# Delta-rule core: the next round's setup inside this round's tail, and other homes in PSUM

## What is computed

```
G = cumsum(g);  decay = where(incl, exp(G_i - G_j), 0)
kb = k * beta
a = where(strict, (kb @ k^T) * decay, 0)
rhs = concat[v * beta, kb * exp(G)]
u, w = solve((I + a), rhs)            # unit lower triangular
intra = (q @ k^T) * decay
step:  v_new = u - w @ state
       o = (q * exp(G)) @ state + intra @ v_new
       state = state * exp(g_last) + k_dec^T @ v_new
```

## Time and profile before

| | |
|---|---|
| median of 3 runs | 2420.59 us (2418.37 to 2424.03) |
| the profiled execution, its own time | 2420.17 us |
| its span | 2418.2 us |
| busy: PE, DVE, ACT, POOL | 1996.5, 928.4, 632.6, 32.5 us |
| the core's four rounds in the span | from 123.5 to about 333 us |
| HBM read | 639.21 MB, 265 GB/s over the span |

### The profile page before, as it was taken

How to read it: one execution, slowest core, us unless ns; L and a number is a source line. 1 busy time by engine, 2 the same in 40 slices (tenths; PEclk the granted TensorE clock), 3 DMA queues, 4 the chain that set the end, 5 groups by cost and what they waited for, 6 DMA issues and landing times.

```text
span 2418.2 us, 34547 instructions
## 1 busy us (share of the span) xinstructions
PE 1996.5 (83%) x14552; PEld 1375.0 (57%) x14552; DVE 928.4 (38%) x1676; ACT 632.6 (26%) x1065; POOL 32.5 (1%) x51
## 2 busy tenths in 40 slices
PE   8887888999988998999987666666999987666665
PEld 7765656887755886988853222222978843222222
DVE  4655563767555566544521000002544521000001
ACT  3321234441124443464420000001364420000000
POOL 0100000000000000000000000000000000000000
PEclk9998899999998999999989888888999978888888
DMA  9301024776954576442559999999542569999997
GB/s 326 118 25 36 2 71 140 253 282 235 362 209 174 199 288 220 167 148 106 229 242 425 427 426 426 427 425 410 215 148 116 218 251 426 426 427 426 426 427 312
DMA packets 150882, 641.86 MB, mean 265 GB/s; under 512 B 9374, under 2 KB 30904, under 8 KB 117622
## 3 DMA queue, kind: packets, MB, share of 16 engines
q1 hardware_dynamic: 144474, 637.13, 66.7%
q10 hardware_dynamic: 6300, 3.20, 0.4%
HBM read 639.21 MB, written 1.10 MB: 265 GB/s over the span
## 4 chain that ended last, share of the span: by engine, by line
PE 57%; DMA 32%; DVE 5%; ACT 2%; issue 1%; DVEq 1%; POOL 0%; SPq 0%; ACTq 0%; POOLq 0%
DMA ring<-in_w_down 32%; PE psum L1321 6%; PE psum L936 5%; PE psum L937 5%; PE psum L938 5%; PE psum L1457 4%; PE psum L691 3%; PE psum L1039 3%; PE psum L1311 2%; PE psum L1200 2%; PE psum L1199 2%; PE psum L1201 2%; PE psum L761 1%; PE psum L1056 1%; PE psum L1190 1%
## 5 line engine op out<-in xcount | busy, mean ns | idle before, releaser
L1437 PE MATMUL psum<-ring,arena 128*32 128x256 f32 x4096 | 292.1, 438 | 168.3 <-DMA ring<-in_w_up 130.7
L1437 PEld LDWEIGHTS psum<-ring,arena 128*32 128x32 f32 x4096 | 143.0, 123 | 319.7 <-issue 144.5
L1457 PE MATMUL psum<-ring,arena 128*32 128x512 f32 x1024 | 162.6, 765 | 96.3 <-DMA ring<-in_w_down 87.5
L936 PE MATMUL psum<-arena_r 128*128 128x512 f32 x512 | 206.3, 403 | 11.8 <-DVE arena_r L1858 7.1
L2262 DVE TENSOR_TENSOR arena<-psum,arena 128x256 f32<-128x256 f32 x32 | 13.6, 425 | 526.4 <-PE psum L1437 526.4
L938 PE MATMUL psum<-ring_r,arena_r 128*128 128x512 f32 x512 | 203.6, 398 | 0.0
L1570 DVE TENSOR_TENSOR ring_r<-ring,arena_r 128x2048 fp32r<-128x2048 f32 x64 | 143.7, 2287 | 85.7 <-ACT arena_r L2334 85.6
L2269 DVE TENSOR_TENSOR arena<-psum,arena 128x512 f32<-128x512 f32 x64 | 44.3, 692 | 269.1 <-PE psum L1457 267.7
L1457 PEld LDWEIGHTS psum<-ring,arena 128*32 128x32 f32 x1024 | 32.6, 125 | 190.2 <-DMA ring<-in_w_down 102.2
L2334 ACT CAST arena_r<-ring 128x2048 fp32r<-128x2048 f32 x64 | 119.5, 1903 | 71.7 <-PE psum L938 71.7
L2755 ACT ACTIVATE arena<-psum 128x256 f32<-128x256 f32 x32 | 12.3, 384 | 479.5 <-PE psum L1437 479.5
(11 more groups left out here) (405 smaller groups left out, 3361.9 us busy)
## 6 DMA issues: line engine op xcount, KB each, us to landing
ring<-in_w_up SPq DMA_DIRECT2D x64, 2048.0 KB, 26.1
ring<-in_w_down SPq DMA_DIRECT2D x64, 2048.0 KB, 26.3
ring<-in_w_gate SPq DMA_DIRECT2D x60, 2048.0 KB, 26.6
ring<-in_mlp_w SPq DMA_DIRECT2D x32, 2048.0 KB, 8.4
ring<-in_w_mod SPq DMA_DIRECT2D x24, 2048.0 KB, 11.1
ring<-in_w_in SPq DMA_DIRECT2D x20, 2048.0 KB, 8.5
ring<-in_gdn_w_in SPq DMA_DIRECT2D x8, 2048.0 KB, 18.3
ring<-in_dswa_w_in SPq DMA_DIRECT2D x9, 1536.0 KB, 13.7
```

Source lines behind the costliest of these rows:

```text
L936: mm(o, xh, wh, start=start, stop=False, skip_group_check=True)
L1437: ins = mm(PS[32 * j:32 * j + 32, 4 + m, 0:T], XG[:, k, 0:CAP] if first else XGE[:, k, :], W(v + 2 * m + u, D)[:, kk, j * T:(j + 1) * T], ...
L1457: ins = mm(PS[32 * j:32 * j + 32, (7, 4)[half], :], HTE[:, k % 2, 32 * (k // 2):32 * (k // 2) + 32], W(v + 4 + u, D)[:, j, half * 512:(hal ...
```

## The change

- Next round's setup is issued inside the tail: the decay products right behind the last large product, ahead of the tail's first; beta rows behind L855's and L881's successors; key products between and behind the tail's products. The key products (128 columns) and the query products (now apart, 128 columns) replace the 256-column ones. `core_done` is no longer waited for by PE.
- Setup lives in banks 4 to 7, the tail in banks 0 to 2, and the small levels in banks 6 and 7. The key products overwrite the decay products' bank once DVE has read them (`dt_in`).
- DVE makes the full key matrix at once (decay times minus beta, then times the products: two instructions of 128x512 per lane), and the masked part is taken out of it by four copies of 32x128. The tile AN and the later `kd_raw` and `kd_beta` go; one 128x512 product with the query products per lane remains (`query_decay`, at q = 0 and 1).
- R1 of the second chunk: v times beta is made early, and one pass of four 128x128 instructions, with a precomputed minus exp(G) times beta per token, replaces the three 128x512 steps. Keys by state are signalled before queries by state are issued.
- Gate steps: from the tail's two places and level q = 3 they move, in rounds 1 to 3, to: two at q = 0, one each at q = 1 and 2, one ahead of the wait for the spread tiles, one behind each P of the large levels, one ahead of the transposes. In round 0 two stand ahead of the first level and three in q = 0 to 2.
- ACT takes the exponents of the next round between the tail's copies.

The diff, cut to its core:

```diff
+            def decay_products(it):
...
+                        ins = mm(pair(4 + l, P)[:, h], GS[:, l, g:g + 1].to_broadcast([P, P]), CUM[:, d, :], start=True, stop=True)
+            def beta_rows(it, l):
...
+                    mm(pair(6 + l, P)[:, h], BT[:, l, g:g + 1].to_broadcast([P, P]), ident, start=True, stop=True)
+            def key_products(it, l):
...
+                pe.wait_ge(sem("dt_in"), 2 * it + l + 1)
...
+            def query_products(it):
...
+                    pe.wait_ge(sem("qs_out"), it)
...
+                small_p(it, 0, 0)
                 if it >= 1:
-                    pe.wait_ge(sem("core_done"), it)
+                    query_products(it)
                     pe.wait_ge(sem("z_act"), it)
...
+                    gate_step(it, 0)
+                small_q(it, 0, 0)
+                small_p(it, 0, 1)
+                gate_step(it, 1 if it else 2)
+                small_q(it, 0, 1)
+                for q in range(1, NSMALL):
...
+                    if q < 3:
+                        gate_step(it, q + (1 if it else 2))
...
+                    if q == NSMALL and it:
+                        gate_step(it, 4)
...
-                    if q == NSMALL:
-                        gate_step(it, 4)
+                    gate_step(it, 5 if q == NSMALL else 7)
...
+                if it < 3:
+                    decay_products(it + 1)
                 pe.wait_ge(sem("u_grown"), (it + 1) * nlev * 2)
                 pe.wait_ge(sem("r1_ready"), 2 * it + 1)
                 for h in range(4):
-                    ins = mm(pair(6, P)[:, h], lanes[fst]["U"][:, h], R1[:, h], start=True, stop=True)
+                    ins = mm(pair(0, P)[:, h], lanes[fst]["U"][:, h], R1[:, h], start=True, stop=True)
                 ins.then_inc(sem("tail_mm"), 1)
-                gate_step(it, 6)
+                if it < 3:
+                    beta_rows(it + 1, 0)
...
+                if it < 3:
+                    key_products(it + 1, 0)
...
-                gate_step(it, 7)
...
+                if it < 3:
+                    beta_rows(it + 1, 1)
...
+                if it < 3:
+                    key_products(it + 1, 1)
...
+            def decays_beta(it, l):
...
+                v.scalar_tensor_tensor(lanes[l]["KD"][:, :, 0], lanes[l]["DT"], -1.0, pair(6 + l, P), ALU.mult, ALU.mult)
+            def begin(it, l):
...
+                v.tensor_tensor(kd[:, :, 0], pair(4 + l, P), kd[:, :, 0], ALU.mult)
+                settle()
+                for r in quads:
+                    v.copy_predicated(sm["U"][r], bm(masks32[r, 1 - d, 0], 4), kd[r, :, 0, r])
+                settle()
+                v.transpose(sm["Tm"].rearrange("p h c -> p (h c)"), sm["U"].rearrange("p h c -> p (h c)")).then_inc(sem("t_ready"), 1)
...
+                if it < 3:
+                    decays(it + 1, 0)
+                    decays(it + 1, 1)
+                    units()
+                dve.wait_ge(sem("tail_mm"), 7 * it + 1)
+                values_beta(d, hs, snd)
...
-                v.tensor_tensor(R1, pair(0, P), eg, ALU.mult)
-                settle()
-                v.tensor_tensor(R1, V[:, hs, snd, :], R1, ALU.subtract)
-                settle()
-                v.tensor_tensor(R1, R1, bc(BT[:, snd, d * 8 + hg:d * 8 + hg + 4], P), ALU.mult).then_inc(sem("r1_ready"), 1)
+                for h in range(4):
+                    ins = v.scalar_tensor_tensor(R1[:, h], pair(0, P)[:, h], NB[:, d, snd, hg + h:hg + h + 1], R1[:, h], ALU.mult, ALU.add)
+                ins.then_inc(sem("r1_ready"), 1)
+                if it < 3:
+                    decays_beta(it + 1, 0)
+                    settle()
+                    begin(it + 1, 0)
...
+                v.tensor_tensor(o, pair(2, P), qs, ALU.add).then_inc(sem("core_done"), 1)
+                if it < 3:
+                    decays_beta(it + 1, 1)
+                    settle()
+                    begin(it + 1, 1)
```

More of the change, by code:

```diff
@@ new lines, in key_products @@
+            def key_products(it, l):
+                hg = (it % 2) * 4
+                pe.wait_ge(sem("dt_in"), 2 * it + l + 1)
+                for h in range(4):
+                    k = KQT[:, hg + h, 0, l * P:(l + 1) * P]
+                    ins = mm(pair(4 + l, P)[:, h], k, k, start=True, stop=True)
+                ins.then_inc(sem("core_setup"), 1)
+            def query_products(it):
+                hg = (it % 2) * 4
+                if it >= 1:
+                    pe.wait_ge(sem("qs_out"), it)
+                for l in range(2):
+                    for h in range(4):
+                        ins = mm(pair(l, P)[:, h], KQT[:, hg + h, 0, l * P:(l + 1) * P], KQT[:, hg + h, 1, l * P:(l + 1) * P],
+                                 start=True, stop=True)
+                ins.then_inc(sem("core_setup"), 1)
@@ new lines, in small_p @@
+            def small_p(it, q, l):
+                if q == 0:
+                    pe.wait_ge(sem("t_ready"), 2 * it + l + 1)
+                else:
+                    pe.wait_ge(sem("t_grown"), (it * 5 + q - 1) * 2 + l + 1)
+                for h in range(4):
+                    for b in range(4):
+                        r = quads[b]
+                        ins = mm(PS[r, 6 + l, h * Q32:(h + 1) * Q32], lanes[l]["KD"][r, h, 0, r], small[l]["Tm"][r, h],
+                                 start=True, stop=True, tile_position=(Q32 * b, Q32 * b))
+                ins.then_inc(sem("p_mm"), 1)
@@ new lines, in small_q @@
+            def small_q(it, q, l):
+                pe.wait_ge(sem("p_out"), (it * nlev + q) * 2 + l + 1)
+                if q >= 1:
+                    pe.wait_ge(sem("u_grown"), (it * nlev + q - 1) * 2 + l + 1)
+                for h in range(4):
+                    for b in range(4):
+                        r = quads[b]
+                        ins = mm(PS[r, 6 + l, P + h * Q32:P + (h + 1) * Q32], small[l]["U"][r, h], small[l]["PP"][r, h],
+                                 start=True, stop=True, tile_position=(Q32 * b, Q32 * b))
+                ins.then_inc(sem("q_mm"), 1)
@@ L778, in _ @@
                 fst, snd = (0, 1) if d == 0 else (1, 0)
+                if it == 0:
+                    gate_step(it, 0)
+                    gate_step(it, 1)
+                small_p(it, 0, 0)
                 if it >= 1:
-                    pe.wait_ge(sem("core_done"), it)
+                    query_products(it)
                     pe.wait_ge(sem("z_act"), it)
[L782 to L794, removed]
@@ L844, in _ @@
                     if q < nlev - 1:
[L845 removed]
+                        gate_step(it, 6)
                         for l in range(2):
@@ L860, in _ @@
                 for h in range(4):
-                    ins = mm(pair(7, P)[:, h], lanes[fst]["Tm"][:, h], VN[:, h], start=True, stop=True)
+                    ins = mm(pair(1, P)[:, h], lanes[fst]["Tm"][:, h], VN[:, h], start=True, stop=True)
                 ins.then_inc(sem("tail_mm"), 1)
@@ L2400, in _, with gate_out, decay_exp @@
             a.activation(KD_S, KD_S, ACT.Exp).then_inc(sem("decay_out"), 1)
+            def gate_out(it):
+                u, t = it // 2, it % 2
+                if t == 0:
+                    act.wait_ge(sem("tok_mm"), u + 1)
+                else:
+                    spent(act, U_Z + u)
+                a.copy(Z[:, t, u * 512:(u + 1) * 512], bank(3)).then_inc(sem("z_act"), 1)
+            def decay_exp(it, l):
+                act.wait_ge(sem("dt_in"), 2 * it + l + 1)
+                a.activation(lanes[l]["DT"], lanes[l]["DT"], ACT.Exp).then_inc(sem("dt_out"), 1)
+            decay_exp(0, 0)
+            decay_exp(0, 1)
             for it in range(4):
-                for l in range(2):
-                    act.wait_ge(sem("dt_in"), 2 * it + l + 1)
-                    a.activation(lanes[l]["DT"], lanes[l]["DT"], ACT.Exp).then_inc(sem("dt_out"), 1)
                 for q in range(NSMALL):
@@ L2428, in _ @@
                 for i in range(2):
[L2429 to L2430 removed]
+                    if i == 1 and it < 3:
+                        decay_exp(it + 1, 1)
+                        gate_out(it)
+                    act.wait_ge(sem("tail_mm"), 7 * it + (1, 6)[i])
+                    a.copy(VN, pair((0, 2)[i], P)).then_inc(sem("vn_out"), 1)
                     if i == 0:
[L2432 to L2433 removed]
+                        if it < 3:
+                            decay_exp(it + 1, 0)
+                        act.wait_ge(sem("tail_mm"), 7 * it + 2)
+                        a.copy(SST, pair(1, P)).then_inc(sem("s_out"), 1)
                         if it == 3:
```

155 lines of the change are left out of this document (67 added, 88 removed).

## The result

| | before | changed |
|---|---|---|
| median of four runs, us | 2419.48 (2412.09 to 2424.03) | 2376.02 (2373.54 to 2382.86) |
| ratio, 95% interval | | 0.984 (0.9822 to 0.9858) |
| profiled execution, us | 2420.17 | 2378.30 |
| its span, us | 2418.2 | 2376.3 |

Of the 41.9, 0.7 came ahead of the core (its first decay product starts at 122.80 in place of 123.50), 39.7 in the core, and the rest, 1.5, behind it.

The account below looks back on a forecast made before the run. The core was taken as bound by a chain of short steps, tail and setup one behind the other, with no engine full. Savings of 26.2 + 8.4 + 2.0 + 2.0 = 38.6 us gave 2382 us, range 2371 to 2397.

Parts of the forecast that it names:

- the last tail: End of the last round: R1 in a single pass after half the key products, 2.0 us saved once.
- Boundaries: Last large update to lane 1 ready, three times: 14.8 us in place of 23.0, the third 15.6; 26.2 saved.
- What ends the boundary: At lane 1 ready: DVE ends last, at 14.8 us; PE just fits, at 14.7, and is late next.
- Round 0: Round 0's setup, not overlapped with a tail: lane 1 ready at the same time, 0 saved, some tenths either way.
- First level: Lane 1 ready to the first level's end: 2.7 us in place of 4.8, 8.4 saved over four rounds.
- Gate steps: Level q = 3 loses one, the last large level gains one: 0 in sum, each end 4.4 us over four rounds.
- Clock: First products of the large levels, slow behind idle: 2.0 us saved, between 6.6 gained and 6.6 lost.
- The swinging clock: Rival: each shorter round loses one more stretch to 1.2 GHz; 30 us saved, 2390; chance 0.10.
- the hidden gain: Rival: the MLP behind the core must wait for its weights, so nothing is gained; 2420; chance 0.03.
- the slower core: Rival: the clock stays low through the core, some 40 us more over four rounds; 2460; chance 0.03.
- PE's instructions come late: Rival: a 1.08 us stall of PE in every level, sixteen times, 17 us given back; 2399; chance 0.06.
- several stalls in a level: Sign of being wrong: several stalls of PE per level in the core.

Follow-up runs that it names:

- a0: The changed kernel itself, unedited, timed again beside the variants as their base: 2378.17 us, ratio 0.9848.
- x1: Changed kernel with the whole setup issued behind the tail again, new homes in PSUM kept: 2399.25 us, ratio 0.9938.
- x3: Changed kernel with all eight gate steps of a round back at the places of the kernel before: 2381.61 us, ratio 0.9855.
- x6: Changed kernel with all gate steps between a large product and its reader moved to level q = 3, the spread-tile wait and ahead of the transposes: 2368.38 us.
- x4: Changed kernel without the gate steps of levels q = 1 and 2, so z is not whole: 2381.21 us, ratio 0.9867.
- x5: Changed kernel with gate step 5 moved from behind the first large product to the wait for the spread tiles: 2370.85 us, ratio 0.9835.

## Why the prediction was right, point by point

The forecast was 2382 with a range of 2371 to 2397; 2376.0 was measured, and 2378.2 in a0. The path that it gave, tail and setup one behind the other, is what the change shortened, and x1 shows it by putting them back. That the core's sum came so close, 39.7 for 38.6, is in part luck: boundaries, levels 1 to 3 and the last tail gave 4.7 us more than forecast, round 0's setup, the first levels and the large levels 3.6 less.

*Boundaries: 26.2 forecast, 28.0 measured.* The timeline of the sum was hit step by step. From the end of the update, forecast and measured: R1 done at 6.9 and 6.75; lane 0 ready at 10.1 and 9.8; the output added at 11.6 and 11.15; lane 1 ready at 14.8 and 14.24. The masked copy of 32x128, the unknown price, came at 1.23 for four, 0.31 each: the row of the nearest shape was right. The forecast gave 0.07 us to each step between dependent steps of DVE, and several overlap by that much instead. Direction 1 needed 14.96 in place of 15.6.

*What ends the boundary.* DVE, as forecast; PE is next, and late by the 0.43 us seen above.

*Round 0: 0 forecast, 1.6 lost.* Its first decay products ran at 1.2 GHz in the first profile (granted clock 0.52 from 122.8 to 126.6 us); the same 16 took 2.02 us in a0, whose setup took 10.97, so the term itself stands.

```profile
122.80 3.76 PE L783 MATMUL psum<-arena 128*128 128x128 f32 x16 [0.56 <-ACT arena L2462]
```

*First level: 8.4 and 7.9.* It takes 2.73, 2.88, 2.87 and 2.73 us, near the 2.7 of the sum.

*Gate steps: 0, with ends of 4.4.* They nearly cancel, but each side was paid otherwise than thought. Level q = 3 lost one, and the levels 1 to 3 gained 2.4 (1.6 in a0) rather than 4.4; stalls grew by 5.1 in the core in the same time, which may be the rest. The large levels got one more, behind the last product and ahead of its reader. Without it x3 and x6 are 0.81 shorter in round 1 (x3 beside a0, x6 beside x5), so it costs some 3.2 us in four rounds.

*Clock: 2.0.* The first product of the large levels, in the chain of waits of the changed kernel, for the earlier trace rows:

```profile
147.78 3.78 PE psum L876 x16
...
190.54 2.10 PE psum L876 x16
...
231.07 2.50 PE psum L876 x16
...
271.08 2.10 PE psum L876 x16
```

Sum 10.48 in place of 13.79: 3.3 gained, and 1.6 lost again in round 0's setup: 1.7 by these rows. The large levels show only 0.5 of it because of the added gate step. In a0 the four took 11.37 in sum, 2.4 gained, so the term rests on where single executions fell. The price of the high clock was too low: 1.79 was read from a product that follows other work, and one that starts behind a wait takes 2.10 or 2.11 in x6 at a granted clock of 1.00. So at most 5.4 could go, not 6.6.

The Trainium skill ("TensorE: Matmul & The Clock Gate", section "A second HAM failure mode: psum-queue depth-cycling") tells of a kernel in which short waits between groups of matmuls keep the clock swinging. x6 doesn't show this: it has PE stalls of 5.2 us in its core, the longest of them 0.89 us, and a granted clock of 1.00 in all four rounds. x4 leans that way: its stalls are 12.4 us, the longest 1.82, and its rounds have 0.86 to 0.92.

*The rivals.* The swinging clock, the hidden gain and the slower core didn't come: in the first profile the clock is 0.86, 1.00, 0.96 and 1.00 for 0.90, 0.90, 0.84 and 0.89. One rival came in part, at a third of its price: PE's instructions come late. It was priced at 1.08 us in every level, 17 us; stalls grew from 2.0 to 7.1. Since the boundaries gave more than forecast, it is not seen in the total. The prediction gave several stalls in a level as a sign of being wrong; nine were counted in all sixteen levels.

The Trainium skill's "Runtime: NRT & Kernel Launch", section "Instruction fetch mechanics", says that an engine's instructions come in blocks of 256, and that crossing into the next is mostly hidden. The trace agrees with the size (254 instructions between stalls) and not with the second: the changed kernel stands 7.1 us of 170 at such places.

## What to carry to other kernels

Where a chain of short steps on two engines is followed by the preparation of the next round, issue that preparation between the chain's steps, on each queue, and check what memory keeps it apart: here the homes in PSUM. The order of filler work is worth tuning after it: put it where an engine stands idle, in front of a wait, and not between a product and its reader on the chain (0.81 us each here, and nothing in the one place where another engine was late anyway). Before taking work out of a stage of many small instructions, look whether the engine stands with nothing to wait for: then the work that goes out may mostly make the stall longer.

## What the runs showed of the hardware

In a stretch of small matmuls (32x32, float32, each with its load) PE did not get through a block of 254 instructions in less than some 3.4 us when such blocks ended in stalls one after another: 3.41 to 3.96 us in the changed kernel, 3.38 to 3.74 in x4 with less work in the block. A level with a gate step has 130 matmuls with as many loads, just over one block, and no run took several in a row much faster than that. A kernel with fewer instructions per level was not run, so what it would gain is open.

A stall may bring the low clock with it. PE in round 2 of the changed kernel stood 2.32 us ahead of the last small product; the large product behind it took 2.69 us where those at the high clock take 2.10:

```profile
228.57 0.50 PE L834 MATMUL psum<-x_normed 32*32 32x32 f32 x32 [2.32 <-issue]
229.00 2.08 PE L761 MATMUL psum<-ring,h_featmajor 128*128 128x512 f32 x2
230.88 2.69 PE L876 MATMUL psum<-arena 128*128 128x128 f32 x16
```

The gate step between them shows it too: 2.08 us for what takes 1.12 elsewhere. The granted clock is 0.64 from 228 to 231 us. At the same place a0 stood 2.32 us and x5 2.05, and that round's clock was 0.92 and 0.96; x6 stood 0.79 and kept 1.00.
